# Wider first matmuls, two units by halves, and a reordered head of a two-block fp32 kernel

## What is computed

```python
h = rmsnorm(x, norm_mix)                 # (1, 256, 2048)
p = h @ w_in                             # 2048 x 4352
h_fwd, h_bwd = implicit_filters(...)     # h = sin(fr1*(feat@w1+b1)); h = sin(fr2*(h@w2+b2)); h @ w3
y_b = hyena_mixer(p[..., a:b], ...)      # xs = dwconv3(xb); x0,x1,v = split(xs); z = x1*v; long convolution of z
...
x = x + concat(y_a, y_b, y_c) @ w_out
# then: rmsnorm, gated feed-forward with dwconv3; then attention, a squared-relu MLP, norms
```

## Time and profile before

| what | value |
|---|---|
| median of three runs | 2182.36 us |
| the profiled execution | 2182.6 us, of which the span from first to last instruction is 2180.8 us |
| TensorE matmuls, busy | 2171.8 us, 100% |
| VectorE | 1306.2 us, 60% |
| ScalarE | 1009.5 us, 46% |
| GpSimd | 52.1 us, 2% |
| DMA, mean | 189 GB/s; 332 GB/s in the first fortieth of the span |
| chain that ended last | TensorE 96%, DMA 1%, VectorE 1%, ScalarE 1% |

### The profile page before, as it was taken

One profiled execution on the slowest core, in us unless ns is written; L12 is line 12 of the kernel. 1 busy time (PEld: TensorE's weight loads), 2 busy tenths in 40 slices (PEclk: granted clock), 3 DMA queues, 4 the chain that ended last, 5 costly groups with the idle time before them and its releaser, 6 DMA issues.

```text
span 2180.8 us, 27986 instructions
## 1 busy us (share of the span) xinstructions
PE 2171.8 (100%) x11714; PEld 1865.5 (86%) x11714; DVE 1306.2 (60%) x1613; ACT 1009.5 (46%) x1182; POOL 52.1 (2%) x76
## 2 busy tenths in 40 slices
PE   9999999999999999999999999999999999999999
PEld 8888888888888888888898889878888888888887
DVE  7868557776777775444655665456555555444445
ACT  6444446545545554333655444445433344334443
POOL 1030000000000000000001010000000000000000
PEclk9999999999999999999999999999999999999999
DMA  9655656555555555555566555546666665555552
GB/s 332 204 179 165 221 174 201 186 194 193 193 186 184 191 176 208 185 186 191 163 206 201 156 173 194 193 135 213 190 185 188 191 193 187 185 190 191 193 191 99
DMA packets 268718, 412.41 MB, mean 189 GB/s; under 512 B 6901, under 2 KB 246709, under 8 KB 249904
## 3 DMA queue, kind: packets, MB, share of 16 engines
q1 hardware_dynamic: 265152, 397.30, 55.7%
q0 software_dynamic: 2432, 11.74, 1.5%
q10 hardware_dynamic: 1008, 1.58, 0.2%
HBM read 408.48 MB, written 2.11 MB: 188 GB/s over the span
## 4 chain that ended last, share of the span: by engine, by line
PE 96%; DMA 1%; DVE 1%; ACT 1%; issue 0%; SPq 0%; DVEq 0%; ACTq 0%
PE bank L1422 34%; PE bank L1438 18%; PE bank L1467 11%; PE bank L1462 11%; PE bank L1463 11%; PE bank L1425 2%; PE bank L1426 2%; PE bank L1440 2%; DMA raw<-in_w_in 1%; PE bank L1318 1%; PE bank L1276 0%; ACT whi L420 0%; DVE M L1191 0%; PE bank L1345 0%; PE bank L1400 0%
## 5 line engine op out<-in xcount | busy, mean ns | idle before, releaser
L720 DVE TENSOR_TENSOR wlo<-raw,whi 128x2048 fp32r<-128x2048 f32 (+1 forms) x373 | 854.6, 2293 | 783.6 <-ACT whi L420 783.2
L420 ACT ACTIVATE whi<-raw 128x2048 fp32r<-128x2048 f32 (+1 forms) x373 | 714.0, 1916 | 794.3 <-PE bank L1467 436.4
L1422 PE MATMUL bank<-hh,whi 128*128 128x512 f32 x3392 | 823.6, 395 | 2.2 <-DVE hh L737 1.1
L1422 PEld LDWEIGHTS bank<-hh,whi 128*128 128x128 f32 x3392 | 625.6, 189 | 132.9 <-DVE hh L737 1.6
L1438 PEld LDWEIGHTS bank<-hh,wlo 128*128 128x128 f32 x3392 | 429.5, 188 | 18.0 <-DVE wlo L720 0.9
L1438 PE MATMUL bank<-hh,wlo 128*128 128x256 f32 x3392 | 434.9, 281 | 0.1
L1462 PE MATMUL bank<-whi,hh 128*128 128x512 f32 x1072 | 422.4, 394 | 0.0
L1463 PE MATMUL bank<-whi,hh 128*128 128x512 f32 x1072 | 421.2, 393 | 0.0
L1467 PE MATMUL bank<-wlo,hh 128*128 128x512 f32 x1072 | 270.3, 394 | 0.0
L1462 PEld LDWEIGHTS bank<-whi,hh 128*128 128x128 f32 x1072 | 201.5, 188 | 47.4 <-DVE M L788 0.2
L1467 PEld LDWEIGHTS bank<-wlo,hh 128*128 128x128 f32 x1072 | 201.3, 188 | 46.7
(11 more groups left out here) (233 smaller groups left out, 907.7 us busy)
## 6 DMA issues: line engine op xcount, KB each, us to landing
raw<-in_mlp_w SPq DMA_DIRECT2D x128, 1024.0 KB, 5.4
raw<-in_ffn_w_up SPq DMA_DIRECT2D x88, 1024.0 KB, 5.1
raw<-in_ffn_w_down SPq DMA_DIRECT2D x44, 1024.0 KB, 4.8
raw<-in_w_in SPq DMA_DIRECT2D x33, 1024.0 KB, 5.8
raw<-in_fox_w_in SPq DMA_DIRECT2D x32, 1024.0 KB, 5.4
raw<-in_fox_w_in SPq DMA_DIRECT2D x16, 1032.0 KB, 5.4
raw<-in_w_out SPq DMA_DIRECT2D x16, 1024.0 KB, 4.8
raw<-in_fox_w_out SPq DMA_DIRECT2D x16, 1024.0 KB, 4.7
```

What stands on the lines that cost most here:

```text
L420: e.activation(whi[i % RING][:, 0:n], raw[i % RAW][:, 0:n], ACT.Copy).then_inc(s_hi, 1)
L720: e.tensor_tensor(wlo[i % RING][:, 0:n], raw[i % RAW][:, 0:n], whi[i % RING][:, 0:n].bitcast(F), ALU.subtract).then_inc(s_lo, 1)
L1422: e.matmul(bank[b][:, :], wh[:, k, s], hh[:, kk, :], start=kk == 0, stop=False)
```

## The change

- TensorE's first matmuls on ones: 13 of 512 columns in place of 32 of 128.
- Unit 0: the high part of its second quarter is made by VectorE (`tensor_copy`) and not by ScalarE, with a semaphore of its own. VectorE's order of `low` and low parts changes.
- Units 1 and 2 are loaded, and their high parts made, in two halves; unit 1's low part too. TensorE waits for halves.
- `cols` is issued behind the first piece of X. The second copy of x goes to other columns of M (`gx0`) and is loaded after unit 4. GpSimd's first three small loads wait for unit 1's first half and not for all of it.
- Groups 0 and 1 leave the loop and are written out by hand on ScalarE and VectorE: the banks of group 0, then (behind the root) those of group 1 are emptied before `rb` exists; the products by `rb`, the taps and the folded product follow. `conv` is cut into `convolved`, `times_r` and `outer_taps`, `middle_tap` into `convolved` and `middle_tap`.
- The spread moves from the side of unit 3 to that of unit 4, ahead of filter2. The second sine moves from the side of unit 5 to that of unit 6, which on ScalarE stands behind the middle taps of group 2. In group 2 both engines split unit 8 between `convolved` and the rest.
- The steps of `sine` between the angle and the clamp, with the clamp, move from VectorE to GpSimd (`turns_off`), each fused step as two instructions. GpSimd loads `w3`, `decay`, `ft` and `skips` after the first of the two and after the squares, and `cs` after the second.

```diff
-    0: [("angles", 0)], 1: [("filter1", 0), ("first_root", 0)], 3: [("spread", 0)], 4: [("filter2", 0), ("angles", 1)], 5: [("sin", 1)],
-    7: [("filter3", 0)],
+    1: [("filter1", 0)], 4: [("spread", 0), ("filter2", 0)], 6: [("sin", 1)], 7: [("filter3", 0)],
...
@@ sync @@
-            load(1)
+            load_halves(1)
...
-            load(2)
+            load_halves(2)
             load(3)
+            load(4)
             for h in range(2):
-                e.dma_start(gx[:, h, :], A["xt"][:, h, :]).then_inc(s_xh[h], 16)
-            for i in range(4, NU):
+                e.dma_start(gx0[:, h, :], A["xt"][:, h, :]).then_inc(s_xh[h], 16)
+            for i in range(5, NU):
...
@@ gpsimd @@
+            def turns_off(n):
+                at = 8 * n
+                e.wait_ge(s_angle, n + 1)
+                e.tensor_scalar(fn, fa, 1.0 / (2 * math.pi), MAGIC, ALU.mult, ALU.add).then_inc(s_sine, 1)
+                e.wait_ge(s_sine, at + 1)
+                e.tensor_scalar(fn, fn, -MAGIC, None, ALU.add).then_inc(s_sine, 1)
+                for i, c in enumerate(TWO_PI):
+                    e.wait_ge(s_sine, at + 2 + 2 * i)
+                    e.tensor_scalar(fh, fn, -c, None, ALU.mult).then_inc(s_sine, 1)
+                    e.wait_ge(s_sine, at + 3 + 2 * i)
+                    e.tensor_tensor(fa, fa, fh, ALU.add).then_inc(s_sine, 1)
+                e.wait_ge(s_sine, at + 8)
+                e.tensor_scalar(fa, fa, 3.1415925, -3.1415925, ALU.min, ALU.max).then_inc(s_fa, 1)
...
-            e.wait_ge(s_raw[1], 16)
+            e.wait_ge(s_wh[0], 16)
             e.dma_start(ident[:, :], A["ident"]).then_inc(s_id, 16)
...
-            e.wait_ge(s_unit, 3)
-            for dst, src in ((w3, A["w3"]), (CS, A["cs"])):
-                e.dma_start(dst, src).then_inc(s_const, 16)
-            e.dma_start(decay, A["decay"][:, :, 0:384]).then_inc(s_decay, 16)
+            turns_off(0)
             e.wait_ge(s_lx, 16)
             e.wait_ge(s_sqx, 2)
+            e.dma_start(w3, A["w3"]).then_inc(s_const, 16)
+            e.dma_start(decay, A["decay"][:, :, 0:384]).then_inc(s_decay, 16)
             e.dma_start(FT, A["ft"]).then_inc(s_ft, 16)
             e.dma_start(skips, A["skip_row"]).then_inc(s_ft, 16)
+            turns_off(1)
+            e.dma_start(CS, A["cs"]).then_inc(s_const, 16)
...
@@ scalar @@
+                if q == 1:
+                    continue
...
-            done[0] = 1
-            split(1)
+            high_half(1, 0)
+            high_half(1, 1)
             for q in range(4, 8):
                 e.wait_ge(s_x[2 + q // 2], 16)
                 high(q, "mix")
+            high_half(2, 0)
+            high_half(2, 1)
+            done[0] = 3
+            split(4)
             e.wait_ge(s_col, 16)
+            convolved("x1", 0, 0, group_done(U_IN, 0))
+            for h in range(2):
+                e.wait_ge(s_xh[h], 16)
+                e.activation(gx0[:, h, :], gx0[:, h, :], ACT.Square, accum_out=ss_x[:, h:h + 1]).then_inc(s_sqx, 1)
+            root(1, rstd)
+            convolved("v", 0, 2, group_done(U_IN, 1))
+            sine(0)
+            split(6)
+            middle_tap("x1", 0)
+            middle_tap("v", 0)
             for g, (kind, j, _) in enumerate(IN_GROUPS):
+                if g < 2:
+                    continue
...
+                    convolved(kind, j, b, group_done(U_IN, g))
+                    if g == 2:
+                        split(i + 4)
+                    middle_tap(kind, j)
...
@@ vector @@
+            low(0, "mix")
+            e.wait_ge(s_w0[1], 16)
+            e.tensor_copy(whi[0][:, quarter[1]], raw[0][:, quarter[1]]).then_inc(s_hi0v, 1)
...
+            angles(0)
+            e.wait_ge(s_hih, 2)
+            split(3)
+            convolved("x1", 0, 0, group_done(U_IN, 0))
+            split(4)
+            e.wait_ge(s_sqx, 2)
+            root(1, ss_x, 1.0 / D, RMS_EPS, rstd)
+            e.wait_ge(s_rcp, 1)
+            e.wait_ge(s_id, 16)
+            diagonal(rstd)
+            convolved("v", 0, 2, group_done(U_IN, 1))
+            spread_out(1)
+            angles(1)
+            times_r("x1", 0)
+            split(5)
+            times_r("v", 0)
+            outer_taps("x1", 0)
+            split(6)
+            outer_taps("v", 0)
+            folded_product(0)
...
@@ tensor @@
-            for _ in range(32):
-                e.matmul(bank[7][:, 0:P], onesr[:, :], onesr[:, :], start=True, stop=True)
+            for _ in range(13):
+                e.matmul(bank[7][:, :].rearrange("p (a b) -> p a b", a=4), onesr[:, :], onesr[:, :].unsqueeze(1).to_broadcast([P, 4, P]),
+                         start=True, stop=True)
```

More of the change, by code:

```diff
@@ L459, in small_terms, with convolved @@
                 return e.activation(dst, bank[b][:, T:2 * T], ACT.Copy)
-            def middle_tap(kind, j, pair, done):
+            def convolved(kind, j, pair, done):
                 cg = CONV[kind, j]
@@ L467, in middle_tap @@
                     small_terms(pair + n, conv_tiles(kind, j, n)[3]).then_inc(s_cvs, 1)
-                if cg == 0:
-                    split(4)
-                    sine(0)
+            def middle_tap(kind, j):
+                cg = CONV[kind, j]
                 for n in range(2):
@@ L492, in side @@
                 for what, n in SIDE.get(i, ()):
[L493 to L498, removed]
+                    if what == "up_r":
                         root(3, r_up)
@@ L988, in side @@
                 for what, n in SIDE.get(i, ()):
-                    if what == "first_root":
-                        e.wait_ge(s_sqx, 2)
-                        root(1, ss_x, 1.0 / D, RMS_EPS, rstd)
-                        e.wait_ge(s_rcp, 1)
-                        e.wait_ge(s_id, 16)
-                        diagonal(rstd)
-                    elif what == "up_r":
+                    if what == "up_r":
                         e.wait_ge(s_ss, 2)
@@ L1010, in side @@
                         e.tensor_scalar(v_2, v_2, RMS_EPS, None, ALU.mult).then_inc(s_rr, 1)
-                    elif what == "angles":
-                        sine(4 + n, col("filt", 2 * n, 64), col("filt", 2 * n + 1, 64))
                     elif what == "filter3":
@@ L1103, in vector, with low_part @@
             e.wait_ge(s_gmix, 16)
-            for q in range(4):
-                s = slice(512 * q, 512 * q + 512)
-                e.wait_ge(s_x[q], 16)
-                low(q, "mix")
-                e.wait_ge(*((s_hi0, q + 1) if q < 3 else (s_hi, 1)))
-                e.tensor_tensor(wlo[0][:, s], raw[0][:, s], whi[0][:, s].bitcast(F), ALU.subtract).then_inc(s_lo0 if q < 3 else s_lo, 1)
-            done[0] = 1
-            split(1)
+            def low_part(u, s):
+                return e.tensor_tensor(wlo[u][:, s], raw[u][:, s], whi[u][:, s].bitcast(F), ALU.subtract)
+            quarter = [slice(512 * q, 512 * q + 512) for q in range(4)]
+            e.wait_ge(s_x[0], 16)
+            low(0, "mix")
+            e.wait_ge(s_w0[1], 16)
+            e.tensor_copy(whi[0][:, quarter[1]], raw[0][:, quarter[1]]).then_inc(s_hi0v, 1)
+            e.wait_ge(s_w0[0], 16)
+            e.wait_ge(s_hi0, 1)
+            low_part(0, quarter[0]).then_inc(s_lo0, 1)
+            e.wait_ge(s_x[1], 16)
+            low(1, "mix")
+            e.wait_ge(s_x[2], 16)
+            low(2, "mix")
+            e.wait_ge(s_hi0v, 1)
+            low_part(0, quarter[1]).then_inc(s_lo0, 1)
+            e.wait_ge(s_x[3], 16)
+            low(3, "mix")
+            e.wait_ge(s_hi0, 2)
+            low_part(0, quarter[2]).then_inc(s_lo0, 1)
+            e.wait_ge(s_hi, 1)
+            low_part(0, quarter[3]).then_inc(s_lo, 1)
+            e.wait_ge(s_hih, 1)
+            low_part(1, slice(0, 1024)).then_inc(s_loh, 1)
+            e.wait_ge(s_hi, 2)
+            low_part(1, slice(1024, 2048)).then_inc(s_lo, 1)
+            done[0] = 2
             for q in range(4, 8):
@@ L1115, in vector @@
             e.wait_ge(s_col, 16)
+            angles(0)
[18 more added lines that the diff above has]
+            folded_product(0)
             for g, (kind, j, _) in enumerate(IN_GROUPS):
+                if g < 2:
+                    continue
                 i, b = U_IN + 2 * g, 2 * (g % 2)
-                group(i, ahead=g and (kind, j) != ("gu", 2))
+                group(i, ahead=g > 2 and (kind, j) != ("gu", 2))
                 if kind in ("x1", "v", "x0"):
-                    conv(kind, j, b, group_done(U_IN, g))
-                    if kind == "v":
-                        for n in range(2):
-                            e.wait_ge(s_cv2, 4 * CONV[kind, j] + 3 + n)
-                            e.tensor_tensor(cx[:, n, :], cx[:, n, :], cx[:, 2 + n, :], ALU.mult).then_inc(s_zm, 1)
-                        for n in range(2):
-                            late, early, folded = cx[:, n, P:T], cx[:, n, P - 1::-1], z[:, 2 * j + n, :]
-                            e.wait_ge(s_zm, 2 * j + n + 1)
```

(9 more changed lines are left out.)

81 lines of the change are left out of this document (50 added, 31 removed).

## The result

| kernel | median | lowest to highest | runs |
|---|---|---|---|
| before | 2182.38 us | 2182.20 to 2182.49 | 4 |
| after | 2194.49 us | 2194.12 to 2195.11 | 4 |

A forecast was written before the change was run, and what follows sets the result against it. TensorE, busy 2171.8 of 2180.8 us, was taken as the bound, so only filter3's start counted: 56.4 + 2.9 = 59.3 against 57.33, giving 2182.36 + 2.0 = 2184.4 us, range 2180.6 to 2186.4.

The forecast's parts named there:

- The front: TensorE up to unit 7: unit 1 starts 1.1 us sooner, unit 5's wait goes, filter3 could start 2.2 us sooner.
- VectorE's list: VectorE's work from the spread's copy to group 2's first product, ahead of the second sine: 17.1 us, ending at 55.0.
- the forecast's 56.4: Start of filter3 behind two ScalarE taps and the second sine, before GpSimd's turns are counted; 0.9 us of gain remains.
- First chain: GpSimd's first nine full-turn steps, from about 21: sine 0 ready by some 33, cost nothing.
- I count one of nine as free: 2.9 us: GpSimd's second chain takes turns with VectorE by whole instructions and delays its gapless list by 2.9 us, bounds 0 and 4.2.
- the 59.3 forecast: Forecast start of filter3: 56.4 plus 2.9 for GpSimd's turns, 2.0 us later than 57.33.
- Rival C: VectorE wins every turn; GpSimd's second chain ends at 62, cs late too: 5.3 to 9.7 us later, 2187.7 to 2192; chance 0.12.
- F: The start of filter3, the quantity forecast; 57.33 us before.
- B: GpSimd slips in between VectorE's instructions at 0 to 1 us: 2181.4 us, from 2180.7 to 2182.4; chance 0.24.
- The rest of the program shifts with it: From filter3 on TensorE follows itself, so the total moves by as much as filter3's start.
- Rival A: Turns between GpSimd and VectorE taken in full: 2184.4 us, from 2183.2 to 2185.7; chance 0.46.

The follow-up runs named there:

- table ahead: The kernel after, with the cs table issued before GpSimd's second chain instead of behind it: 2190.37 us, 1.0036 times before.
- pause filled: The kernel after, with 36 matmuls of 512 columns that nobody reads ahead of filter3's waits: 2189.43 us, 1.0031 times before.
- chain on VectorE: The kernel after, with the second chain back on VectorE as six instructions behind the second angles, cs issued with the other tables: 2184.61 us.
- reordered: The kernel after, second chain on VectorE, low parts of units 5 to 7 and second sine moved ahead: 2180.76 us, again 2180.74; 0.9992 times before.
- sine late: The reordered kernel with ScalarE's second sine put back behind the middle taps of group 2: 2187.21 us, 1.0021 times before.
- short copies, PSUM: The kernel after, with 14 one-column copies out of a PSUM bank between VectorE's long instructions: 2188.16 us, 1.0027 times before.
- short copies, SBUF: The kernel after, with 14 one-column copies from an SBUF column between VectorE's long instructions: 2187.84 us, 1.0025 times before.
- short products: The kernel after, with 14 one-column products of two SBUF columns between VectorE's long instructions: 2188.69 us, 1.0030 times before.
- front alone: The kernel before, with only wide first matmuls, units 1 and 2 by halves and first copies shared with VectorE: 2182.24 us, 0.9999 times before.

## Why the prediction was wrong

In one table, by the starts of filter3 and of unit 9 (us) in each profile, and the profiled time:

| kernel | filter3 | unit 9 | between | profiled time |
|---|---|---|---|---|
| before | 57.33 | 65.74 | 8.4 | 2182.6 |
| after | 63.96 | 77.48 | 13.5 | 2194.4 |
| table ahead | 60.73 | 73.32 | 12.6 | 2190.4 |
| pause filled | 63.85 | 72.24 | 8.4 | 2189.3 |
| chain on VectorE | 58.98 | 67.39 | 8.4 | 2184.5 |
| reordered | 55.24 | 63.66 | 8.4 | 2180.7 |
| sine late | 57.54 | 70.82 | 13.3 | 2188.0 |
| short copies, PSUM | 59.23 | 72.41 | 13.2 | 2189.4 |
| short copies, SBUF | 59.31 | 69.30 | 10.0 | 2186.4 |
| short products | 60.23 | 71.87 | 11.6 | 2189.0 |

- **The front, right.** Unit 0 at 7.03 (7.0 forecast), unit 1 at 14.02 (14.0), spread 37.16 (37.2), units 5, 6, 7 at 38.26, 43.91, 49.51 (38.3, 43.9, 49.5), no wait at unit 5, filter3 possible at 55.3 (55.1). Each comes out of rows of before plus one gap removed, and each is within 0.2 us.
- **VectorE's list, right.** From 37.8 to 55.0, forecast as 17.1 us ending at 55.0, and ScalarE's middle taps end at 56.2. A sine of 0.4 us behind them would give the forecast's 56.4 to within 0.2 us; no run has this order without the chain.
- **First chain, right in cost.** It ran from 21.10 to 34.43, not to 33, and its sine at 34.75 did not wait.
- **"I count one of nine as free: 2.9 us", wrong.** This is the step that failed. The forecast read from the earlier trace rows that the two engines hold each other up by whole instructions. That is so, but it then let them take turns. In this list they do not: VectorE lost 0.3 us, three of nine steps were done when it ended, and the chain was over at 60.02, not within 1 us of VectorE's end. One long hold-up was in the earlier trace rows: GpSimd waited 2.2 us there, for one instruction. The rows could not say who is next after it. Where short instructions stand in between, turns are taken, but they cost VectorE 2.0 us and not 2.9. That filter3 starts at 59.23 there, beside the 59.3 forecast, is luck: 1.0 us of it is the added instructions.
- **Rival C, right in the main.** It had the second chain unserved until VectorE stands still near 57, its end at 62, and `cs` behind it. Measured: end at 60.02, table at 63.9, F at 63.96, inside its 62.6 to 67. The end near its 62 is in part luck: three steps had been served early, and the last five took 0.8 us each from start to start, where C had 0.5 to 0.7. It was given 0.12, and the small losses seen on VectorE (0.11 and 0.16) were put down to B as a sign of cheap turns. They fit VectorE winning as well.
- **The clock, priced at nothing.** "The rest of the program shifts with it" holds for a pause only if TensorE comes back at the clock at which it left. By C's own rule a filter3 at 63.96 makes 2182.36 + 6.6 = 2189.0 us, and that is what the kernel with the filled pause takes (2189.4). The 5.1 us on top are the clock, and they put the result beyond even C's 2192. Rival A would have paid too, as far as the short instructions show: there filter3 starts at 59.2 to 60.2, and the runs took 2186.2 to 2190.3 us, not 2184.4.
- **The Trainium skill's rule** ("SBUF — State Buffer", section "SBUF: two separate sides"), that whoever starts first has the port pair for its whole instruction while the other is blocked, agrees with the way in which VectorE is held up beside short instructions: 0.94 where 0.46 is free. The same page of the Trainium skill, in its section "Who interferes with whom", has the order of issue decide who is blocked. For the step that began at 43.86 and took 8.71 us the trace disagrees: by its recorded start it was there ahead of the thirteen instructions that VectorE began from 43.9 to 51.7, and each of them went first.

## What to carry to other kernels

Work put on GpSimd beside a VectorE list that has no gap isn't work beside it: if nobody waits for it, it costs little (0.3 us of VectorE's list here), and if somebody does, count its end as the end of VectorE's list plus the steps that are left (55.4 and 60.0 here). Price a new pause of TensorE twice, once by its length and once for the lower clock behind it, and look first for what can be moved so that the pause doesn't open. Before work is moved to another engine, look at the due times on its own: here three `split` calls and one sine in another order, with the chain back on VectorE, took the kernel from 2184.61 to 2180.76 us.

## What the runs showed of the hardware

- A GpSimd step on 64x256 elements, 0.84 to 0.91 us when free, took 8.71 us beside a VectorE train of long two-input instructions, which lost about 0.3 us in 15.7. One-column instructions in the train (0.07 us each), with SBUF or PSUM sources, one or two of them, brought the nine steps' end from 60.0 to 50.9 to 51.9.
- The same step takes 0.28 to 0.29 us on VectorE (39.02 to 41.30 with the chain there), a third of GpSimd's.
- Pauses of TensorE of 2.04, 2.33, 2.47, 5.22 and 8.67 us were each followed by a stretch at 1.2 GHz; those of 1.17 us (front alone) and 0.91 to 1.27 us (within unit 7, with short instructions) had none of their own. The clock can fall after the pause is over: with short copies from SBUF it fell at 61.5, 2.2 us after filter3's start. The stretch lasted from 3.4 to 17 us and cost 1.6 to 5.1, and its length did not go by that of the pause: behind one and the same pause of 2.47 us it was 3.4 us in one kernel and 10.2 in another.
- With wide first matmuls the clock rose sooner. The profile's granted clock reads 1.00 from the start of the program, so here the level is read from the spacing of the matmuls: a matmul of 512 columns takes 0.43 us in the stretch at 0.50 behind filter3 in after (from 69.35) and 0.23 at 1.00. In after the last eight of them took 3.45 us from 3.29 on, 0.43 each, and unit 0's first four only 1.20 in all, so the rise lies close to unit 0's start. In the kernel with short copies from PSUM, whose first 6 us are the same program, the same eight took 2.54, so it lies among them. In the kernel before, the first five of unit 0 still took 0.43 each, to 10.3 us.
